# Differential attention in a two-block transformer: small products placed inside the units, score products in pairs, maps weighed and scaled by VectorE

## Reference, cut to what matters

```python
def diff_attention(x, w_qkv, q_g, k_g, lq1, lk1, lq2, lk2, sub_g, w_o, rel_bias, lambda_init):
    qkv = x @ w_qkv
    q, k, v = jnp.split(qkv, 3, axis=-1)
    q = rms_norm(q.reshape(B, S, N_HEADS, 2, HEAD_DIM), q_g) * (HEAD_DIM ** -0.5)
    k = rms_norm(k.reshape(B, S, N_HEADS, 2, HEAD_DIM), k_g)
    v = v.reshape(B, S, N_HEADS, V_DIM)
    ...
        logits = jnp.einsum('bhcqd,bhckd->bhcqk', q_blk, k).astype(jnp.float32)
        logits = logits + bias[None, :, None]
        logits = jnp.where(dist >= 0, logits, -jnp.inf)
        probs = jax.nn.softmax(logits, axis=-1)
        w = probs[:, :, 0] - lam * probs[:, :, 1]
        return jnp.einsum('bhqk,bhkd->bhqd', w.astype(v.dtype), v)
    ...
    o = rms_norm(o, sub_g) * (1.0 - lambda_init)
    return o.reshape(B, S, N_HEADS * V_DIM) @ w_o
```

## Time and profile before

| | |
|---|---|
| median of 3 executions | 2559.6 us (2558.55 to 2559.84) |
| profiled execution, its own time | 2563.97 us |
| its span | 2562.2 us |
| mean granted clock of TensorE | 0.994 |
| TensorE busy | 2485.8 us (97% of the span) |
| VectorE, ScalarE, POOL busy | 1357.0, 1054.1, 1137.3 us |
| the section of the change | 649.67 to 882.04 us |

### The profile page before, as it was taken

The page is one execution under the profiler, slowest core; times in us unless marked ns, Lnnn a source line. Parts: engine busy times, 40 slices in busy tenths (PEclk is TensorE's granted clock), DMA queues, the critical chain, the costliest instruction groups (busy, mean ns, idle before and its releaser), DMA issues.

```text
span 2562.2 us, 32133 instructions
## 1 busy us (share of the span) xinstructions
PE 2485.8 (97%) x11898; PEld 1986.2 (78%) x11898; DVE 1357.0 (53%) x2122; ACT 1054.1 (41%) x1443; POOL 1137.3 (44%) x586
## 2 busy tenths in 40 slices
PE   7989999999899999999999999999999999999998
PEld 4658888888676788888876877888888757888887
DVE  6975644644445566366346664652544464652453
ACT  5564322235566642223334253532334443532333
POOL 5844445444343444444443423444444313444443
PEclk9999999999999999999999999999999999999999
DMA  5215546524222265464343312324323121324322
GB/s 147 67 58 159 186 145 191 181 88 117 82 58 75 58 181 181 139 197 161 96 121 107 99 50 73 84 77 112 99 73 100 62 66 51 84 80 119 92 83 67
DMA packets 398713, 273.50 MB, mean 107 GB/s; under 512 B 10195, under 2 KB 381907, under 8 KB 398588
## 3 DMA queue, kind: packets, MB, share of 16 engines
q1 hardware_dynamic: 384764, 221.52, 30.2%
q10 hardware_dynamic: 13824, 50.34, 5.3%
HBM read 269.70 MB, written 2.12 MB: 106 GB/s over the span
## 4 chain that ended last, share of the span: by engine, by line
PE 81%; ACT 6%; DVE 5%; POOL 5%; issue 2%; SPq 0%; DMA 0%; DVEq 0%; ACTq 0%; POOLq 0%
PE ps L716 25%; PE ps L718 24%; PE ps L717 24%; POOL act L2441 2%; POOL weight_lo L2398 2%; ACT weight_hi L2542 1%; DVE act L1998 1%; PE ps L1420 1%; PE ps L1062 1%; PE ps L1036 1%; PE ps L1024 1%; ACT arena L2880 1%; PE ps L1021 1%; DVE tmp L1826 1%; DVE u_lo L1592 0%
## 5 line engine op out<-in xcount | busy, mean ns | idle before, releaser
L2398 POOL TENSOR_TENSOR weight_lo<-weight_raw,weight_hi 128x1024 fp32r<-128x1024 f32 (+4 forms) x418 | 947.7, 2288 | 1247.9 <-ACT weight_hi L2542 1245.9
L718 PE MATMUL ps<-u_hi,weight_lo 128*128 128x512 f32 (+1 forms) x2456 | 931.3, 379 | 0.0
L716 PE MATMUL ps<-u_hi,weight_hi 128*128 128x512 f32 (+1 forms) x2248 | 881.4, 392 | 18.2 <-DVE u_lo L1524 8.0
L717 PE MATMUL ps<-u_lo,weight_hi 128*128 128x512 f32 (+1 forms) x2248 | 870.5, 387 | 0.0
L2542 ACT ACTIVATE weight_hi<-weight_raw 128x2048 fp32r<-128x2048 f32 (+2 forms) x215 | 366.9, 1707 | 576.5 <-PE ps L718 540.8
L718 PEld LDWEIGHTS ps<-u_hi,weight_lo 128*128 128x128 f32 x2456 | 463.3, 189 | 87.5
L716 PEld LDWEIGHTS ps<-u_hi,weight_hi 128*128 128x128 f32 x2248 | 424.0, 189 | 124.6 <-issue 20.6
L717 PEld LDWEIGHTS ps<-u_lo,weight_hi 128*128 128x128 f32 x2248 | 424.1, 189 | 87.8 <-issue 3.3
L718 PE MATMUL ps<-act_hi,weight_lo 128*128 128x512 f32 (+1 forms) x748 | 281.6, 376 | 0.0
L716 PE MATMUL ps<-act_hi,weight_hi 128*128 128x512 f32 (+1 forms) x704 | 270.1, 384 | 2.6 <-DVE act_lo L1493 2.6
L717 PE MATMUL ps<-act_lo,weight_hi 128*128 128x512 f32 (+1 forms) x704 | 269.3, 382 | 0.0
(11 more groups left out here) (345 smaller groups left out, 2795.4 us busy)
## 6 DMA issues: line engine op xcount, KB each, us to landing
weight_raw<-in_ffn_w_up SPq DMA_DIRECT2D x132, 512.0 KB, 5.2
arena<-in_ada_w ACTq DMA_DIRECT2D x96, 512.0 KB, 5.8
weight_raw<-in_ffn_w_down SPq DMA_DIRECT2D x64, 704.0 KB, 4.6
weight_raw<-in_ffn_w_gate SPq DMA_DIRECT2D x44, 512.0 KB, 4.0
weight_raw<-in_ev_w_in SPq DMA_DIRECT2D x10, 1024.0 KB, 5.3
weight_raw<-in_conv_w_pw SPq DMA_DIRECT2D x16, 512.0 KB, 5.6
weight_raw<-in_ple_w_gate SPq DMA_DIRECT2D x16, 512.0 KB, 3.8
weight_raw<-in_attn_w_qkv SPq DMA_DIRECT2D x16, 512.0 KB, 5.2
```

Source lines behind the costliest of these rows:

```text
L716: pe.matmul(bank, w[0], x[0], start=start, stop=False)
L717: pe.matmul(bank, w[0], x[1], start=False, stop=False)
L718: return pe.matmul(bank, w[1], x[0], start=False, stop=stop)
L2398: low_part = pool.tensor_tensor(w_lo[r][:, cols], raw[r][:, cols], w_hi(k0 + j)[:, cols].bitcast(F32), ALU.subtract)
```

## The change

- TensorE: the functions `one_unit_turn`, `two_unit_turn` and `last_values_turn` call the small work from inside a unit (`between`, after a step k of a tile, or after a half b of a value tile). `score_pair` issues both components of a block behind one wait for both maxima of the block before, and the components have banks 4 and 5 for their own. The weighing of an even turn's head moves into tile 0 of the next odd turn's unit.
- VectorE: `mix` makes four mixes on the unscaled maps and then four scalings; the ratio of row sums goes into the factor of the second map. The order of copies, normed, logits and value copies is another.
- ScalarE: roots stand ahead of the split in odd turns, and between two pairs of exponentials in even turns.
- POOL: `normalise` is gone; in its place POOL waits for `mixed`.

```diff
         def score_bank(b, comp):
-            return 4 + (2 * b + comp) % 3
+            return 4 + comp
...
-                def score_pairs(g, blocks):
-                    if blocks[0] == 0:
+                def score_pair(g, b):
+                    if b == 0:
                         pe.wait_ge(qk_normed, 2 * g + 2)
-                    for b in blocks:
-                        for comp in range(2):
-                            item = 2 * b + comp
-                            if item >= 3:
-                                pe.wait_ge(max_done, 8 * g + item - 2)
-                            elif g > 0:
-                                pe.wait_ge(max_done, 8 * g - (1, 0, 2)[item])
+                    if g or b:
+                        pe.wait_ge(max_done, 8 * g + 2 * b)
+                    for comp in range(2):
...
+                def one_unit_turn(i):
+                    def between(tile, k):
+                        if (tile, k) == (0, 2) and i >= 3:
+                            weigh(i - 3)
+                        if (tile, k) == (0, DC - 1) and i >= 2:
+                            turn(i - 2, (0, 1))
+                        if (tile, k) == (1, 2) and i >= 2:
+                            turn(i - 2, (2, 3))
+                        if (tile, k) in ((1, 3), (1, 4), (1, 6)):
+                            score_pair(i - 1, (3, 4, 6).index(k))
+                    unit(f"qk{i}", between)
...
+                    score_pair(i - 1, 3)
+                    if i >= 2:
                         weigh(i - 2)
+                    if i >= 3:
                         stat(i - 3)
+                    head_sums(i)
+                def two_unit_turn(i):
+                    def between_qk(tile, k):
+                        if (tile, k) == (0, DC - 1):
+                            turn(i - 2, (0, 1))
+                        if (tile, k) == (1, 3):
+                            turn(i - 2, (2, 3))
+                    def between_v(tile, b):
+                        if (tile, b) == (0, 0):
+                            score_pair(i - 1, 1)
+                            head_sums(i)
+                        if (tile, b) == (0, 1):
+                            score_pair(i - 1, 2)
+                        if (tile, b) == (1, 0):
+                            score_pair(i - 1, 3)
+                    unit(f"qk{i}", between_qk)
+                    if i >= 3:
+                        stat(i - 3)
+                    score_pair(i - 1, 0)
+                    unit(f"v{i // 2 - 1}", between_v)
+                def last_values_turn():
+                    def between(tile, b):
+                        if (tile, b) == (0, 1):
+                            turn(G - 2, (0, 1))
+                        if (tile, b) == (1, 0):
+                            turn(G - 2, (2, 3))
+                            score_pair(G - 1, 0)
+                    unit("v3", between)
+                    for b in range(1, NB):
+                        score_pair(G - 1, b)
+                    weigh(G - 2)
+                    stat(G - 3)
...
-                    link(dve.tensor_scalar(rowinv[:, 4:8], rowinv[:, 4:8], lam[:, 6:7], None, ALU.mult))
+                    link(dve.scalar_tensor_tensor(rowinv[:, 4:8], rowinv[:, 4:8], lam[:, 6:7], rowsum[:, 0:4], ALU.mult, ALU.mult))
...
-                        dve.wait_ge(scaled, s0 + 4 * g + b + 1)
-                        dve.scalar_tensor_tensor(probs("diff", g, 0, b), probs("diff", g, 1, b), rowinv[:, 4 + b:5 + b],
-                                                 probs("diff", g, 0, b), ALU.mult, ALU.add).then_inc(mixed, 1)
+                        m = probs("diff", g, 0, b)
+                        link(dve.scalar_tensor_tensor(m, probs("diff", g, 1, b), rowinv[:, 4 + b:5 + b], m, ALU.mult, ALU.add), 0 if b == NB - 1 else 1)
+                    for b in range(NB):
+                        m = probs("diff", g, 0, b)
+                        dve.tensor_scalar(m, m, rowinv[:, b:b + 1], None, ALU.mult).then_inc(mixed, 1)
...
-            def normalise(g):
...
                         if i >= 1:
-                            normalise(i - 1)
+                            pool.wait_ge(mixed, 4 * i)
...
+                roots(0)
+                split_after("qk0", Step(0))
...
+                    if i % 2:
+                        exps(i - 1, (0, 1, 2))
+                        key_square(i)
+                        exps(i - 1, (3,))
+                        roots(i)
+                        if i >= 2:
+                            weighed_square(i - 2)
+                        split_after(f"qk{i}", Step(0))
+                    else:
+                        key_square(i)
+                        split_after(f"qk{i}", Step(0))
                         exps(i - 1, (0, 1))
+                        roots(i)
                         exps(i - 1, (2, 3))
+                        split_after(f"v{i // 2 - 1}", Step(0))
```

More of the change, by code:

```diff
@@ L1089, in qkv_attention, with unit @@
                 x0 = n.take(x_ready, DC)
[L1090 removed]
+                l0, q0 = n.take(ln_done, G), n.take(squared, G)
                 m0, c0 = n.take(mixed, 4 * G), n.take(o_copied, G)
                 n.take(exp_done, 8 * G)
[L1094 removed]
+                def unit(name, between=lambda i, step: None):
                     t0 = stages[name][2]
@@ L1199, in out_chunk @@
                             mm.then_inc(tile_done, 1)
-                for i in range(G + 3):
-                    for name in head_units(i):
-                        unit(name)
+                def one_unit_turn(i):
[9 more added lines that the diff above has]
+                    unit(f"qk{i}", between)
                     if i == 1:
@@ new lines, in last_values_turn @@
+                def last_values_turn():
[10 more added lines that the diff above has]
+                    stat(G - 3)
+                    for k in range(G - 3):
+                        out_chunk(k)
@@ L1230, in qkv_attention @@
+                unit("qk0")
+                head_sums(0)
+                for i in range(1, G):
+                    (one_unit_turn if i % 2 else two_unit_turn)(i)
+                last_values_turn()
+                turn(G - 1, (0, 1))
+                turn(G - 1, (2, 3))
+                weigh(G - 1)
+                stat(G - 2)
+                out_chunk(G - 3)
+                for k in range(3):
+                    out_chunk(k, 1)
+                stat(G - 1)
                 for k in range(3, G - 2):
@@ new lines, in normed @@
+                def normed(i):
+                    for t, gain in ((0, "q_norm_g"), (1, "k_norm_g")):
+                        dve.wait_ge(qk_root, 2 * i + t + 1)
+                        dve.scalar_tensor_tensor(q_chunk(8 * t + i), q_chunk(8 * t + i), pcol(gain), rinv[t],
+                                                 ALU.mult, ALU.mult).then_inc(qk_normed, 1)
+                query_out(0)
+                key_out(0)
+                for i in range(1, G + 1):
+                    if i % 2 and i >= 3:
+                        weighed_out(i - 3)
+                    if i < G:
+                        query_out(i)
+                    if i >= 2:
@@ new lines, in qkv_attention @@
+                    reciprocals(i - 1)
+                    if i < G:
+                        mix(i - 1)
+                    if i % 2 and i >= 2 or i == G:
+                        weighed_out(i - 2)
+                    elif i % 2 == 0:
+                        values_out(i // 2 - 1, 1)
+                mix(G - 1)
+                turned_out(G - 1, 0)
+                turned_out(G - 1, 3)
+                finish(G - 3)
+                weighed_out(G - 1)
+                finish(G - 2)
+                finish(G - 1)
@@ new lines, in qkv_attention @@
+                query_square(0)
+                key_square(0)
+                roots(0)
+                split_after("qk0", Step(0))
+                for i in range(1, G):
+                    if i % 2 and i >= 3:
+                        weighed_square(i - 3)
+                    if i >= 2:
+                        turned_out(i - 2, 1)
+                    query_square(i)
+                    if i >= 2:
+                        turned_out(i - 2, 2)
+                    if i % 2:
[3 more added lines that the diff above has]
+                        roots(i)
+                        if i >= 2:
+                            weighed_square(i - 2)
+                        split_after(f"qk{i}", Step(0))
+                    else:
+                        key_square(i)
+                        split_after(f"qk{i}", Step(0))
@@ new lines, in qkv_attention @@
+                turned_out(G - 2, 1)
+                turned_out(G - 2, 2)
+                exps(G - 1, range(NB))
+                sc.wait_ge(tile_done, stages["v3"][2] + 2)
+                for g in range(G - 3):
+                    finished(g)
+                split_after("v3", Step(0))
+                weighed_square(G - 2)
+                weighed_log(G - 3)
+                weighed_root(G - 3)
```

(3 more changed lines are left out.)

214 lines of the change are left out of this document (91 added, 123 removed).

## The result

The changed kernel takes 2565.8 us (median of 12 executions, 2563.7 to 2567.5), the kernel before 2560.0 on the same chip: 5.9 us longer, ratio 1.0022, interval 1.0014 to 1.0029. The forecast was 2562.4 (+2.8) in a range of 2551 to 2571.

A forecast was written before the change was run, and what follows sets the result against it. TensorE, busy for nearly all of the section, bounds it. Turns sum +1.9 - 5.7 - 1.8 - 1.8 + 3.8 = -3.6, clock falls add 6.4: +2.8 on the median of 2559.6 gives 2562.4 us, range 2551 to 2571, its own 2557 to 2569.

The forecast's parts named there:

- The weighing's stall of 2.1: Tile 0 of turns 3, 5 and 7: TensorE waits 2.1 us each for VectorE's value copy; 0 to 5 by bounds.
- Turn 1's stall: First score pair of turn 1 waits 2.0 us, as VectorE's norms meet POOL's low halves.
- Turn 8's +3.8: Turn 8 grows from 21.39 to 25.2 us: 2.9 stall and 2.7 waits, less 1.65 and 0.2 saved.
- four pairs take 0.32 + 0.60 + 0.75 + 1.00 = 2.67: One head's paired score products on TensorE take 2.67 us, saving 1.65 per head; bounds 2.1 and 3.9.
- Some 60 more switches [...] cost nothing: TensorE's added switches between products and small work cost 0; a bound of 0.1 each would be 6 us.
- the waits between pairs: Turns 2 to 7: score pairs wait for maxima of the pair before, together 0.85 us per two turns.
- Four falls at 1.6: Clock drops behind turn 8's stall and three of the other four new stalls, adding 6.4 us.
- the likeliest case: The forecast itself, 2562.4 us, chance 0.48: same 0.31, slower 0.17.
- The pairs did overlap: Rival that pairs don't overlap: each head keeps 3.87 us instead of 2.67, giving 2572; chance 0.05.
- held: Rival: clock holds at all stalls of 2.1 and less, turn 8's costs nothing more, giving 2556.0 us; chance 0.15.
- fell everywhere: Rival: clock falls at all five stalls and turn 8's two waits of 1.35, +9.2, giving 2568.8 us; chance 0.18.
- in time: Rival: shorter chains and different norm and POOL meetings remove stalls; two thirds of -14.8 taken, giving 2549 us; chance 0.14.

The follow-up runs named there:

- the first edit: Changed kernel with VectorE copying the second value tile ahead of the reciprocals in even turns, not behind mix and scalings: 2558.3 us, ratio 0.9992 to the kernel before.
- the kernel of both edits: Changed kernel with the value copy ahead of the reciprocals and ScalarE's split ahead of roots(0): 2553.0 us, ratio 0.9968.
- two of its three parts taken alone: Kernel before with the score pairs alone: 2578.2 us, ratio 1.0071; kernel before with VectorE's scaling alone: 2573.7 us, ratio 1.0048.
- the two with three banks: Value copy and split edits plus head 7's scores in three rotating banks, a wait per product: 2552.8 us; that with two switches fewer per odd turn: 2552.6 us.

## Why the prediction was right, and where not

- **Turn 8, turn 1 and the chains.** The weighing's stall of 2.1 was right in place, releaser and size (2.05, 2.16, 2.16), and the first edit showed it causal. Turn 1's stall was 2.43 for 2.0, the head sums' wait 0.66 for 0.9. The scalings took 1.27; I took 1.0, and the copy was priced right. Turn 8's +3.8 came out as +3.6 from other parts: its first pair stalled for 0.71 and not 2.9, since the first norm began ahead of POOL's low half (843.28 against 843.80) and only the second met it; the waits between the pairs were 2.64 with the second pair's 0.65. That makes 1.5 with the savings of 1.65 and 0.2. The pairs' own length, about 1.0 over the 2.67 (next point), and a fall of the clock, 1.2, make up the rest, so that the total came out right by luck. VectorE's two norms and POOL's two low halves in turn 8:

```profile
843.28 3.54 DVE L2040 SCALAR_TENSOR_TENSOR act<-act,par,tmp 128x512 f32<-128x512 f32 x2
...
843.80 5.27 POOL L2479 TENSOR_TENSOR weight_lo<-weight_raw,weight_hi 128x1024 fp32r<-128x1024 f32 x2 [24.44 <-ACT weight_hi L2617]
```

- **Turns 2 to 7** were each too hopeful: 51.8, 52.7 and 52.7 forecast without the clock, 53.6, 55.97 (with one fall of 1.7) and 54.3 measured. The step that failed is "four pairs take 0.32 + 0.60 + 0.75 + 1.00 = 2.67" together with "Some 60 more switches [...] cost nothing". The pairs hold TensorE for 0.42 + 0.63 + 0.84 + 1.05 = 2.94 (starts 771.00, 772.32, 774.54, 776.59 to what follows, rows below), and each costs 0.2 more at its edges, so 3.7 a head, 2.1 more for two. The overlap itself was whole, since a single product held TensorE as long as a pair (0.41 and 0.63 for 128 and 256 columns); the bound of 2.1 for a whole overlap was too low. Against that the transposes became 0.25 a head cheaper, and the waits between pairs came to 0.24, not 0.85. That makes 1.0 of the 1.6 to 1.8 that two turns are long by. Another 0.3 is the stall: the stretch from the head sums of turn 6 to those of turn 7, which holds the third stall, took 35.95 and is 33.54 without it, 2.41 where the chain gave 2.1. The last 0.3 or so I did not follow. The bound of 0.1 a switch that the text named and set aside would have given the size, but not the place: the weighing's products cost nothing at their edges. The second, third and fourth pair of turn 5, each with what follows:

```profile
772.32 0.70 PE L1136 MATMUL ps<-act 64*128 64x256 f32 x4
772.95 0.50 PE L715 MATMUL ps<-u_hi,weight_hi 128*128 128x512 f32 x1
...
774.54 0.92 PE L1136 MATMUL ps<-act 64*128 64x384 f32 x4
775.39 0.50 PE L715 MATMUL ps<-u_hi,weight_hi 128*128 128x512 f32 x1
...
776.59 1.13 PE L1136 MATMUL ps<-act 64*128 64x512 f32 x4 [0.23 <-DVE small L1978]
777.64 1.13 PE L1161 MATMUL ps<-act,arena 128*128 128x512 f32 x2
```

- **The clock.** Four falls at 1.6 were taken; three came, in turns 1, 5 and 8. The one in turn 1 cost 3.2, twice my price, because the clock stayed low for about twice as long (3.57 x 0.45 + 3.00 x 0.50 = 3.1 by the windows above, against 3.77 x 0.45 = 1.7 in turn 5); why it stayed low is open, TensorE had no pause in it. About 1.2 is left for turn 8 by the comparison with the kernel of both edits, whose turn 8 took 23.8. That fall did not come behind the norm's stall, where I had put it, but at the last pair, behind waits of 0.65, 0.86 and 1.13:

```profile
855.30:858.70 3.40, 3.40 (x8) 1.28 (x5) 1.51 (x6) 1.98 (x7) 0.00 (x0) 0.51 0.00 0
```

The sum, 6.1, is near my 6.4 by compensation, which is luck. Of the three idles of 2.1 one made a fall and two did not, in one execution, so an idle of one length has both outcomes, as the 1.63 and the 1.67 had.
- **The sum**: without the clock I forecast -3.6 and got about 0: 5.0 too hopeful in turns 2 to 7, 1.4 too dark in turn 8. With the clock it was +2.8 against +5.9. The number lies in the range and in the forecast's own one, 2557 to 2569. The kernel is slower by a little more than the 5.1 us that I called distinguishable: the likeliest case, in the part of it that I had counted as slower. The pairs did overlap, the clock neither held nor fell everywhere, and the chains were not in time.
- **Slips in the sums**, none of which moves the forecast: the chain of the weighing adds up to 16.2 and not 16.1; "falls everywhere" names five stalls and two waits and takes eight times 1.6; "in time" comes to 2549.7.
- **Left open**: why the edges of a score product cost 0.2. Half the rows, or the change of tile shape, would explain it; I varied only how many such places there are.

## What to carry to other kernels

When small work is moved in among the products of the engine that bounds, its own price still counts (the score products' edges took about 1.1 us a head of what the overlap gave), and who must now be ready earlier counts as much. Follow each semaphore that the moved instruction waits for back to the place in the releasing engine's program, and look at what stands ahead of it there: one copy that stood behind a mix cost 7.5 us, one split behind the roots of query and key 4.8, and with both put in front the change turns from 5.9 slower to 7.8 faster than the kernel before (2553.0 against 2560.8, timed side by side). Judge the parts of such a change together, since two of its three parts taken alone cost 18 and 14 us.

## What the hardware showed beside that

- A second score product on the other half of the array's rows is free beside the first (0.42 for two, 0.41 for one), while each place in which such products stand among whole-array products costs about 0.2. A place with whole-array products costs 0.01 to 0.03 (three more cost 0.03, two fewer gave 0.05).
- Idles of TensorE of 1.63 and 1.67 in the second block drop the clock in some executions and not in others (behind the 1.67 in two of the thirteen profiles, behind the 1.63 in three, to 0.61 to 0.66 over 5 us; 1.00 behind both in the rest). The groups of the run times lie 3 to 5 us apart (2559 and 2564 for the kernel before). Single executions move by that much without any edit there, and a median of few with them, so a section's own windows decide what an edit did.
- Short waits close together were no safer for the clock than one of twice their length. The waits of 0.71, 0.65, 0.86 and 1.13 in turn 8 stand in eight of the thirteen profiles, and in six of these the clock went to the lower of its two levels at the last two of them; in the two with three banks, where 0.71 and 0.22 are left, it stayed at 1.00. The idles of 2.05 and 2.16 in turns 3, 5 and 7 made a fall in two of six cases.
- VectorE's norms and mixes, which read two tensors from SBUF, took turns with POOL's low halves, an instruction each: two norms, 1.40 together, took 4.45, and a mix of 0.74 took 2.81 when POOL was 0.07 earlier. VectorE's copies of 512 columns out of PSUM kept their 0.68 beside the same low halves, in some 40 cases of this section, all profiles taken together.
